# The dt projection with two products per tile, unit 0 taking tiles of h along with it, and three units' weights split ahead of dt's chain

## The chip, the cores and the metric

The kernel runs on one core of one Trainium2 chip. The metric is device time in microseconds (us) for one execution, taken as the median over runs. Engines are named as in the profile: PE (TensorE, matrix products), DVE (VectorE), ACT (ScalarE), POOL (GpSimd) and SP (SyncE, which issues most loads).

## The reference

The program is a trunk of two layers on x of shape 512 tokens by 1024 features, float32. Layer 0 mixes tokens with a Mamba-2 state-space scan, layer 1 with a short gated convolution; each is followed by a gated ConvFFN. Only the start of layer 0 is touched here:

```python
h = rms_norm(x, mix_pre_g[0])
zxbcdt = h @ w_in                       # z | x | B | C | dt (32 heads)
xbc = silu(causal_dwconv(x|B|C, conv_w, conv_b))      # 4 taps
dt = softplus(dt_raw + dt_bias)
a_cs = cumsum(dt * -exp(a_log))         # per head, within chunks
lmat = exp(tril(a_cs_l - a_cs_s))
y = C (B^T x dt)*lmat + C prev * exp(a_cs)            # 8 groups of 4 heads
out = rms_norm((y + x * d) * silu(z)) @ w_out
```

Float32 accuracy is kept by splitting both operands of a large product into a float32r high part and the float32r rest: `three` adds high by high, weight rest by high, and high by h's rest.

## The kernel before

All engines run their own instruction stream, written out by hand; semaphores tie them together, and the order in each stream is the order of the code. Weights are cut into **units** of 128 output columns (or 128 input rows). For each unit SP loads `w_raw` (two buffers), ACT copies it to the high part `w_hi` and DVE subtracts to get the rest `w_lo` (`splits_to(n)` on both engines brings the split up to unit n-1; three slots). PE then runs `unit(u)`: 8 tiles k of h, three products each, into one bank of PSUM, so 24 products of 128x512. SP loads unit u only when `w_lo` of unit u-2 is done.

**The start.** ACT and DVE normalise x (`xn_tok`), PE turns it into feature-major tiles in banks 0 to 5 (`turn_xn`), ACT writes `h_hi` per tile k, DVE `h_lo`. PE then does the dt projection (32 columns of weights, padded with zeros to 128 in `wdt_hi` and `wdt_lo`, three products per tile, bank 7), then unit 0, then unit 1.

**dt's chain.** ACT copies dt's rows out (`dt_row`); `turn_dt` on PE transposes them into token-major form; DVE and ACT compute softplus and a (`dt_u` to `a_tok`, ACT with Abs, Exp and Ln); `turn_acs` on PE multiplies by a triangle to form the cumulative sums; ACT copies them (`acs_row`) and stores them to DRAM; SP loads them back as `acs_b`, the same row on all partitions.

**Group 0.** Units 0 to 5 of a group are B, C, two tiles of x and two tiles of z. For B, C and x, `conv_in` (ACT) copies the bank out and writes the first tap, `conv` (DVE) adds three taps, `conv_out` (ACT) applies Silu. `segments` (DVE) forms the differences of the cumulative sums in `mask`, `exps` (ACT) takes Exp of them, `exps_row` (ACT) Exp of `acs_b` into `e_row`. `mask` times `cbm` on DVE waits for all 7 Exp instructions of the group. PE turns x tiles to token-major form after the Silu of each (L1013), DVE makes `xdt` and `xdd` of them, and PE forms the states from `xdd` (L1020), runs the scan (L1030) and goes on with units 6 and 7. Exp and Silu use different tables of ACT, and the compiler puts an ACT_TABLE_LOAD where the function's table changes.

In unit's argument `behind`, a function is given that PE runs after tile k:

```python
            unit(0, bank[GROUP_BANKS[0]][:], behind={1: turn_dt, 3: turn_pages})
            pe.wait_ge(dt_row_done, 1)
            unit(1, bank[GROUP_BANKS[1]][:], behind={2: turn_acs})
```

Of the kernel before, what the change touches and what calls it, by code (L numbers as in the profile page):

```python
# [5 lines left out]
F32 = mybir.dt.float32  # L6
F32R = mybir.dt.float32r
ALU = mybir.AluOpType
# [7 lines left out]
def build(nc, x, mix_pre_g, mix_post_g, ffn_pre_g, ffn_post_g, ssd_w_in, ssd_conv_w, ssd_conv_b,  # L16
# [129 lines left out]
    SC_BANKS = (2, 3, 4, 5, 6, 7)  # L146
    AHEAD = 3

    acs_dram = nc.dram_tensor("acs_dram", [HEADS, T], F32, kind="Internal").ap()

    ctx = ExitStack()
    with ctx:
        def sb(name, shape, dt=F32, stack=ctx):
            return stack.enter_context(nc.sbuf_tensor(name, shape, dt))
# [28 lines left out]
        with ExitStack() as ssd:  # L183
            acs_b = sb("acs_b", [P, HG, T], stack=ssd)
            mask = sb("mask", [P, HG, T], stack=ssd)
            feat = sb("feat", [P, 4, T], stack=ssd)
            pad = sb("pad", [P, 2, T + P], stack=ssd)
            cbm = sb("cbm", [P, T], stack=ssd)
            b_tok = sb("b_tok", [P, LATER], stack=ssd)
            xdt = sb("xdt", [P, C, HG * HD], stack=ssd)  # L190
            xdd = sb("xdd", [P, C - 1, HG * HD], stack=ssd)
            prev = sb("prev", [P, C - 1, HG * HD], stack=ssd)
            e_row = sb("e_row", [P, XG, LATER], stack=ssd)
            z_act = sb("z_act", [P, XG, T], stack=ssd)
            square, total = sb("square", [P, 2, T], stack=ssd), sb("total", [P, T], stack=ssd)
            few = sb("few", [P, P], stack=ssd)
            decay, c_decay = (few[:, n * HG * C:n * HG * C + HG * (C - 1)].rearrange("p (h c) -> p h c", h=HG) for n in range(2))
            d_col = few[:, 2 * HG * C:2 * HG * C + IT]
            acs_tok, dt_tok = sb("acs_tok", [P, C, HEADS], stack=ssd), sb("dt_tok", [P, C, HEADS], stack=ssd)
            with ExitStack() as late:  # L200
                y_hi, y_lo = sb("y_hi", [P, IT, T], F32R, late), sb("y_lo", [P, IT, T], F32R, late)
            with ExitStack() as start:
                xn_tok = sb("xn_tok", [P, C, D], stack=start)
                pages = sb("pages", [P, 4, P], stack=start)
                wdt_raw = sb("wdt_raw", [P, DT, HEADS], stack=start)
                wdt_hi, wdt_lo = sb("wdt_hi", [P, DT, P], F32R, start), sb("wdt_lo", [P, DT, P], F32R, start)
                dt_row = sb("dt_row", [HEADS, T], stack=start)
                a_log_b, dt_bias_b, d_b = (sb(n, [P, HEADS], stack=start) for n in ("a_log_b", "dt_bias_b", "d_b"))
                sum_sq, r_tok = sb("sum_sq", [P, C], stack=start), sb("r_tok", [P, C], stack=start)
                dt_u, dt_e, a_tok = (sb(n, [P, C * HEADS], stack=start) for n in ("dt_u", "dt_e", "a_tok"))  # L210
                acs_row = sb("acs_row", [HEADS, T], stack=start)

        with ExitStack() as rest:
# [23 lines left out]
            sem(n) for n in ("xn_ready", "xn_turned", "page1_turned", "pages_turned", "par1_done", "par_done"))  # L237
        wdt_cleared, wdt_split, dt_row_mm, dt_row_done = (sem(n) for n in ("wdt_cleared", "wdt_split", "dt_row_mm", "dt_row_done"))
        dt_mm, dt_act, dt_vec, acs_mm, acs_row_done, acs_tok_done, pads_done = (
# [83 lines left out]
        def _(pool):  # L323
# [7 lines left out]
                               pattern=[[1, P]], channel_multiplier=-1).then_inc(consts_done, 1)  # L331
            for part in (wdt_hi, wdt_lo):
                pool.memset(part[:].bitcast(F32)[:, :, HEADS:], 0.0).then_inc(wdt_cleared, 1)
            pool.memset(ones[:], 1.0).then_inc(consts_done, 1)
            pool.memset(total[:], 0.0).then_inc(summed, 1)
            for n in range(IT - 1):
# [5 lines left out]
        def _(act):  # L342
# [22 lines left out]
            act.wait_ge(page1_turned, 1)  # L365
            nc.scalar.copy(par[:, 1, 0:ROWS[1]], bank[6][:, 0:ROWS[1]]).then_inc(par1_done, 1)
            act.wait_ge(par1_done, 1)
            for k in range(DT):
                act.wait_ge(xn_turned, k + 1)
                nc.scalar.activation(h_hi[:, k, :], bank[k % 6][:], ACT.Copy, scale=one(col_gain(MIX_PRE, 0, k))).then_inc(h0_hi_done, 1)  # L370
                if k == 0:
                    act.wait_ge(wdt_landed, 16)
                    act.wait_ge(wdt_cleared, 2)
                    nc.scalar.activation(wdt_hi[:, :, 0:HEADS], wdt_raw[:], ACT.Copy).then_inc(wdt_split, 1)
                if k == 3:
                    splits_to(1)
            splits_to(2)
            act.wait_ge(dt_row_mm, 1)
            nc.scalar.copy(dt_row[:], bank[7][0:HEADS, :]).then_inc(dt_row_done, 1)
            act.wait_ge(pages_turned, 1)  # L380
# [11 lines left out]
            nc.scalar.activation(dt_e[:], dt_e[:], ACT.Ln, bias=1.0).then_inc(dt_act, 1)  # L392
            splits_to(3)
            act.wait_ge(acs_mm, 1)
# [35 lines left out]
            for g in range(GROUPS):  # L430
# [5 lines left out]
                conv_in(g, 2, g * XG)  # L436
                if g == 0:
                    exps(g)
                    exps_row(g)
                conv_in(g, 3, g * XG + 1)  # L440
                conv_out(g, 2)
                act.wait_ge(cb_turned, 2 * g + 2)
                nc.scalar.copy(b_tok[:], bank[3][:, 0:LATER]).then_inc(b_tok_done, 1)
                conv_out(g, 3)
                act.wait_ge(unit_done, GU * g + 5)
                nc.scalar.activation(z_act[:, 0, :], bank[0][:], ACT.Silu).then_inc(evicted, 1)
# [131 lines left out]
        def _(dve):  # L578
# [10 lines left out]
            for c in range(C):  # L589
                dve.wait_ge(r_tok_root, c + 1)  # L590
                nc.vector.reciprocal(r_tok[:, c:c + 1], r_tok[:, c:c + 1]).then_inc(r_tok_done, 1)
                dve.wait_ge(r_tok_done, c + 1)
                nc.vector.tensor_scalar(xn_tok[:, c, :], x_tok[:, c, :], r_tok[:, c:c + 1], None, ALU.mult).then_inc(xn_ready, 1)
            dve.wait_ge(par1_done, 1)
            for k in range(DT):
                dve.wait_ge(h0_hi_done, k + 1)
                nc.vector.scalar_tensor_tensor(out=h_lo[:, k, :], in0=bank[k % 6][:], scalar=one(col_gain(MIX_PRE, 0, k)),
                                               in1=h_hi[:, k, :].bitcast(F32), op0=ALU.mult, op1=ALU.subtract).then_inc(h0_lo_done, 1)
                if k == 0:
                    dve.wait_ge(wdt_split, 1)  # L600
                    nc.vector.tensor_tensor(wdt_lo[:, :, 0:HEADS], wdt_raw[:], wdt_hi[:, :, 0:HEADS].bitcast(F32),
                                            ALU.subtract).then_inc(wdt_split, 1)
                if k == 5:
                    splits_to(1)
            splits_to(2)

# [6 lines left out]
            for h in range(HX):  # L613
# [7 lines left out]
                                           op0=ALU.mult, op1=ALU.mult).then_inc(dt_vec, 1)  # L621
            splits_to(3)
            dve.wait_ge(acs_mm, 2)
# [29 lines left out]
            for g in range(GROUPS):  # L653
                conv(g, 0, CONV_T - 2 * GROUPS + g)
                conv(g, 1, CONV_T - GROUPS + g)
                if not g:
                    segments(g)
                conv(g, 2, g * XG)
                conv(g, 3, g * XG + 1)
# [187 lines left out]
        def _(pe):  # L847
# [94 lines left out]
            for c in range(C):  # L942
# [5 lines left out]
                if c == 1:  # L948
                    pe.wait_ge(page1_landed, 16 * N_PAGE1)
                    nc.tensor.transpose(bank[6][:, 0:ROWS[1]], pages[0:ROWS[1], 1, :], ident[0:ROWS[1], 0:ROWS[1]]).then_inc(page1_turned, 1)  # L950
                if c < C - 2:
                    keep_warm(4, 7)

            pe.wait_ge(wdt_split, 2)
            for k in range(DT):
                pe.wait_ge(h0_lo_done, k + 1)
                last = three(bank[7][:], wdt_hi[:, k, :], wdt_lo[:, k, :], h_hi[:, k, :], h_lo[:, k, :], k == 0, k == DT - 1)
                if k + 6 < DT:
                    for c in range(C):
                        turned = turn_xn(k + 6, c)  # L960
                    turned.then_inc(xn_turned, 1)
            last.then_inc(dt_row_mm, 1)

            def turn_dt():
                pe.wait_ge(dt_row_done, 1)
                for c in range(C):
                    last = nc.tensor.transpose(bank[4][:, c * HEADS:(c + 1) * HEADS], dt_row[:, c * P:(c + 1) * P], ident[0:HEADS, 0:HEADS])
                last.then_inc(dt_mm, 1)
# [14 lines left out]

            pe.wait_ge(par1_done, 1)
            unit(0, bank[GROUP_BANKS[0]][:], behind={1: turn_dt, 3: turn_pages})
            pe.wait_ge(dt_row_done, 1)
            unit(1, bank[GROUP_BANKS[1]][:], behind={2: turn_acs})

            for g in range(GROUPS):
                u = GU * g  # L990
                if g:
                    pe.wait_ge(evicted, GU * g)
                unit(u + 2, bank[GROUP_BANKS[2]][:])
                unit(u + 3, bank[GROUP_BANKS[3]][:])
# [142 lines left out]
```

## Time and profile before

| | |
|---|---|
| median of 3 runs | 1345.62 us (1345.48 to 1346.71) |
| profiled execution | 1345.41 us, of which the span of its core 1343.7 us |
| PE busy | 1332.0 us (99% of the span) |
| DVE busy | 784.3 us (58%) |
| ACT busy | 569.2 us (42%) |
| granted TensorE clock | 1.00 (mean of the core) |

Busy time says how long an engine had an instruction in work, averaged over the whole run. The change touches the first 65 us alone, so the stretches there are to be read one by one.

### The profile page before, as it was taken

Reading aid. Unit: us, or ns where it says so; the run is one execution under the profiler, and the core shown is the slowest. Engines: PE = TensorE matmul, PEld = TensorE weight load, DVE = VectorE, ACT = ScalarE, POOL = GpSimd, SP = SyncE. Lnnn points to the kernel's source line nnn. Section 1 sums busy time; section 2 is a strip of 40 time slices with the busy share of each in tenths; the row PEclk is TensorE's granted clock in tenths of the full one; section 3 lists DMA queues with packets and bytes.
Section 4 is the critical chain, followed back from the end, with each engine's and each line's share of the span. In section 5 each row is a group of like instructions: output and inputs, shape, how many; then the busy total and the mean of one; then the engine's idle time right before and its main releaser. Section 6 shows DMA issues by size and latency. Waiting matters only on the chain.

```text
span 1343.7 us, 15929 instructions
## 1 busy us (share of the span) xinstructions
PE 1332.0 (99%) x6474; PEld 1115.5 (83%) x6474; DVE 784.3 (58%) x1139; ACT 569.2 (42%) x875; POOL 24.8 (2%) x28
## 2 busy tenths in 40 slices
PE   8999999999999999999999999999999999999998
PEld 7888888888888988888888888888898888888886
DVE  4889888888525566656542265445566666654223
ACT  6666655566316434333331173222554433333112
POOL 0000000000000000000000000000000000000000
PEclk9999999999999999999999999999999999999999
DMA  5533233432231233333333313334223333333331
GB/s 151 161 110 92 84 107 110 125 110 90 94 125 54 79 95 109 99 103 96 95 125 112 101 55 94 94 99 128 72 69 106 109 94 96 104 99 126 96 108 63
DMA packets 181773, 135.70 MB, mean 101 GB/s; under 512 B 5645, under 2 KB 169893, under 8 KB 180677
## 3 DMA queue, kind: packets, MB, share of 16 engines
q1 hardware_dynamic: 181653, 134.62, 32.8%
q8 instruction: 51, 0.84, 0.2%
q14 instruction: 21, 0.17, 0.0%
q10 hardware_dynamic: 48, 0.07, 0.0%
HBM read 132.51 MB, written 2.16 MB: 100 GB/s over the span
## 4 chain that ended last, share of the span: by engine, by line
PE 97%; ACT 1%; issue 0%; DVE 0%; DMA 0%; SPq 0%; DVEq 0%; ACTq 0%
PE bank L849 21%; PE bank L851 21%; PE bank L850 21%; PE bank L910 9%; PE bank L911 9%; PE bank L912 9%; PE bank L1030 1%; PE bank L1038 1%; PE bank L1020 1%; PE bank L887 1%; PE bank L1013 1%; PE bank L1002 0%; DMA pages<-in_ssd_norm_w 0%; ACT w_hi L355 0%; ACT h_hi L370 0%
## 5 line engine op out<-in xcount | busy, mean ns | idle before, releaser
L849 PE MATMUL bank<-h_hi,w_hi 128*128 128x512 f32 (+1 forms) x1352 | 513.8, 380 | 0.0
L851 PE MATMUL bank<-h_lo,w_hi 128*128 128x512 f32 (+1 forms) x1352 | 511.1, 378 | 0.0
L850 PE MATMUL bank<-h_hi,w_lo 128*128 128x512 f32 (+1 forms) x1352 | 510.8, 378 | 0.0
L585 DVE TENSOR_TENSOR w_lo<-w_raw,w_hi 128x1024 fp32r<-128x1024 f32 x228 | 286.0, 1257 | 325.8 <-ACT w_hi L355 325.8
L355 ACT ACTIVATE w_hi<-w_raw 128x1024 fp32r<-128x1024 f32 x228 | 238.4, 1053 | 195.3 <-PE bank L912 172.3
L851 PEld LDWEIGHTS bank<-h_lo,w_hi 128*128 128x128 f32 x1352 | 254.2, 188 | 47.4
L850 PEld LDWEIGHTS bank<-h_hi,w_lo 128*128 128x128 f32 x1352 | 254.4, 188 | 46.6
L849 PEld LDWEIGHTS bank<-h_hi,w_hi 128*128 128x128 f32 x1352 | 254.3, 188 | 46.4
L910 PE MATMUL bank<-w_hi,hid_hi 128*128 128x512 f32 x416 | 162.4, 390 | 0.0
L912 PE MATMUL bank<-w_hi,hid_lo 128*128 128x512 f32 x416 | 161.9, 389 | 0.0
L911 PE MATMUL bank<-w_lo,hid_hi 128*128 128x512 f32 x416 | 161.8, 389 | 0.0
L912 PEld LDWEIGHTS bank<-w_hi,hid_lo 128*128 128x128 f32 x416 | 78.1, 188 | 16.3
L910 PEld LDWEIGHTS bank<-w_hi,hid_hi 128*128 128x128 f32 x416 | 78.1, 188 | 16.1
L911 PEld LDWEIGHTS bank<-w_lo,hid_hi 128*128 128x128 f32 x416 | 78.1, 188 | 15.9
L780 DVE SCALAR_TENSOR_TENSOR acc<-cpad,par,acc 128x512 f32<-128x512 f32 x104 | 77.9, 749 | 4.4 <-ACT acc L542 1.8
L645 DVE SCALAR_TENSOR_TENSOR feat<-pad,par,feat 128x512 f32<-128x512 f32 x96 | 71.5, 751 | 13.6 <-ACT feat L407 11.3
L546 ACT ACTIVATE acc<-acc 128x512 f32<-128x512 f32 x44 | 27.9, 634 | 115.8 <-DVE acc L780 115.8
L542 ACT ACTIVATE acc<-cpad,par 128x512 f32<-128x512 f32 x44 | 35.9, 817 | 81.9 <-DVE cpad L793 81.9
L549 ACT ACTIVATE hid_hi<-gated 128x512 fp32r<-128x512 f32 x44 | 27.8, 633 | 81.2 <-DVE gated L802 81.2
L785 DVE TENSOR_TENSOR hid_lo<-gated,hid_hi 128x512 fp32r<-128x512 f32 x52 | 36.0, 693 | 36.4 <-ACT hid_hi L549 30.8
L910 PE MATMUL bank<-w_hi,y_hi 128*128 128x512 f32 x128 | 50.3, 393 | 0.0
L912 PE MATMUL bank<-w_hi,y_lo 128*128 128x512 f32 x128 | 49.9, 390 | 0.0
(146 smaller groups left out, 943.9 us busy)
## 6 DMA issues: line engine op xcount, KB each, us to landing
w_raw<-in_ffn_w_up SPq DMA_DIRECT2D x88, 512.0 KB, 3.7
w_raw<-in_ssd_w_in SPq DMA_DIRECT2D x48, 512.0 KB, 3.9
w_raw<-in_ffn_w_down SPq DMA_DIRECT2D x44, 512.0 KB, 3.5
w_raw<-in_sc_w_in SPq DMA_DIRECT2D x24, 512.0 KB, 3.7
acs_b<-acs_dram SPq DMA_DIRECT2D x8, 1024.0 KB, 6.1
w_raw<-in_ssd_w_out SPq DMA_DIRECT2D x16, 512.0 KB, 3.5
w_raw<-in_sc_w_out SPq DMA_DIRECT2D x8, 512.0 KB, 3.5
x_tok<-in_x SPq DMA_DIRECT2D x4, 512.0 KB, 4.9
```

What stands on the lines that cost most here:

```text
L355: nc.scalar.activation(w_hi[slot(u)][:], w_raw[:, u % 2, :], ACT.Copy).then_inc(w_hi_done, 1)
L542: nc.scalar.activation(acc[:], cpad[:, CW - 1:CW - 1 + T], ACT.Identity, bias=one(col_ffn_b(layer, t)), scale=one(col_ffn_w(layer, CW - 1, ...
L585: nc.vector.tensor_tensor(w_lo[slot(u)][:], w_raw[:, u % 2, :], w_hi[slot(u)][:].bitcast(F32), ALU.subtract).then_inc(w_lo_done, 1)
L645: nc.vector.scalar_tensor_tensor(out=feat[:, f, :], in0=pad[:, f % 2, tap:tap + T], scalar=one(col_ssd_w(tap, page_tile)), in1=feat[:, f, ...
L780: nc.vector.scalar_tensor_tensor(out=acc[:], in0=cpad[:, tap:tap + T], scalar=one(cols(tap)), in1=acc[:], op0=ALU.mult, op1=ALU.add).then_ ...
L785: nc.vector.tensor_tensor(hid_lo[:, t, :], gated[:], hid_hi[:, t, :].bitcast(F32), ALU.subtract).then_inc(hid_lo_done, 1)
L849: nc.tensor.matmul(dst, wh, xh, start=start, stop=False)
L850: nc.tensor.matmul(dst, wl, xh, start=False, stop=False)
L851: return nc.tensor.matmul(dst, wh, xl, start=False, stop=stop)
L910: nc.tensor.matmul(dst[:], in_hi[:, k, toks], hi, start=k == 0, stop=False)
L911: nc.tensor.matmul(dst[:], in_hi[:, k, toks], lo, start=False, stop=False)
L912: last = nc.tensor.matmul(dst[:], in_lo[:, k, toks], hi, start=False, stop=k == b.tiles - 1)
```

## The change

- **dt's product.** High part and rest of dt's weights lie side by side in `wdt` (64 columns, no padding). Per tile PE multiplies `wdt` once with `h_hi` and once with `h_lo`: two products with 64 result rows in place of three with 128. `turn_dt` is now a product of the 64 rows of `dt_row` with `pair`, two identities stacked, made on POOL, which adds the two halves while it transposes.
- **Unit 0 with dt.** PE goes over tiles `at` with dt's two products, and does unit 0's three for tile `at - 2` behind them (`LAG = 2`). The first product of a tile waits for `h_hi` of that tile only. `turn_pages` comes before unit 0's last tile, `turn_dt` behind unit 0, and `turn_acs` moves from the third tile of unit 1 to behind the second tile of unit 2.
- **Splits.** dt's weights are split before h; unit 0's weights behind tile 1 of h on both engines (before: ACT behind tile 3, DVE behind tile 5); units 1 and 2 right behind h. Unit 2's split stood behind dt's Ln and a.
- **Order in group 0.** On DVE the taps of the first x tile come before `segments`. On ACT that tile's Silu comes ahead of the second x tile's `conv_in`, `exps` behind it, and `exps_row` behind the second tile's Silu.
- Four of the warming products (`keep_warm`) at the start are dropped.

```diff
@@ gpsimd
-            for part in (wdt_hi, wdt_lo):
-                pool.memset(part[:].bitcast(F32)[:, :, HEADS:], 0.0).then_inc(wdt_cleared, 1)
             pool.memset(ones[:], 1.0).then_inc(consts_done, 1)
+            pool.wait_ge(consts_done, 5)
+            pool.tensor_tensor(pair[:], ident[:, 0:HEADS], ident[:, HEADS:2 * HEADS], ALU.add).then_inc(pair_done, 1)
@@ scalar
+            act.wait_ge(wdt_landed, 16)
+            nc.scalar.activation(wdt[:, :, 0:HEADS], wdt_raw[:], ACT.Copy).then_inc(wdt_split, 1)
             act.wait_ge(par1_done, 1)
             for k in range(DT):
...
-                if k == 0:
-                    act.wait_ge(wdt_landed, 16)
-                    act.wait_ge(wdt_cleared, 2)
-                    nc.scalar.activation(wdt_hi[:, :, 0:HEADS], wdt_raw[:], ACT.Copy).then_inc(wdt_split, 1)
-                if k == 3:
+                if k == 1:
                     splits_to(1)
-            splits_to(2)
+            splits_to(3)
...
             nc.scalar.activation(dt_e[:], dt_e[:], ACT.Ln, bias=1.0).then_inc(dt_act, 1)
-            splits_to(3)
             act.wait_ge(acs_mm, 1)
...
                 if g == 0:
+                    conv_out(g, 2)
+                conv_in(g, 3, g * XG + 1)
+                if g == 0:
                     exps(g)
-                    exps_row(g)
-                conv_in(g, 3, g * XG + 1)
-                conv_out(g, 2)
+                else:
+                    conv_out(g, 2)
...
                 conv_out(g, 3)
+                if g == 0:
+                    exps_row(g)
@@ vector
-                if k == 5:
+                if k == 1:
                     splits_to(1)
-            splits_to(2)
+            splits_to(3)
...
+                conv(g, 2, g * XG)
                 if not g:
                     segments(g)
-                conv(g, 2, g * XG)
                 conv(g, 3, g * XG + 1)
@@ tensor
-                if c < C - 2:
+                if c == 0:
                     keep_warm(4, 7)
...
-                last = three(bank[7][:], wdt_hi[:, k, :], wdt_lo[:, k, :], h_hi[:, k, :], h_lo[:, k, :], k == 0, k == DT - 1)
...
+            for at in range(DT + LAG):
+                if at < DT:
+                    pe.wait_ge(h0_hi_done, at + 1)
+                    nc.tensor.matmul(bank[7][0:2 * HEADS, :], wdt[:, at, :], h_hi[:, at, :], start=at == 0, stop=False)
+                    pe.wait_ge(h0_lo_done, at + 1)
+                    last = nc.tensor.matmul(bank[7][0:2 * HEADS, :], wdt[:, at, :], h_lo[:, at, :], start=False, stop=at == DT - 1)
...
+                if at >= LAG:
+                    k = at - LAG
...
+                    last = three(bank[GROUP_BANKS[0]][:], hi[:, cols], lo[:, cols], h_hi[:, k, :], h_lo[:, k, :], k == 0, k == DT - 1)
...
+                    if at == DT:
+                        turn_pages()
+            pe.wait_ge(dt_row_done, 1)
+            turn_dt()
+
+            unit(1, bank[GROUP_BANKS[1]][:])
...
-                unit(u + 2, bank[GROUP_BANKS[2]][:])
+                unit(u + 2, bank[GROUP_BANKS[2]][:], behind={1: turn_acs} if g == 0 else {})
```

How it moves instructions is shown at three places. First PE at the start, where dt's products meet the tiles of h. Before, three products per tile, then the transposes of a later tile:

```order
L849 MATMUL bank<-h_hi,wdt_hi 128x512
L850 MATMUL bank<-h_hi,wdt_lo 128x512
L851 MATMUL bank<-h_lo,wdt_hi 128x512
L938 MATMUL bank<-ident,xn_tok 128x128 x4
L849 MATMUL bank<-h_hi,wdt_hi 128x512
```

Now, from tile 1 on to tile 3; `wdt` holds dt's weights, `w_hi` and `w_lo` unit 0's:

```order
L984 MATMUL bank<-h_hi,wdt 64x512
L986 MATMUL bank<-h_lo,wdt 64x512
L939 MATMUL bank<-ident,xn_tok 128x128 x4
L984 MATMUL bank<-h_hi,wdt 64x512
L986 MATMUL bank<-h_lo,wdt 64x512
L850 MATMUL bank<-h_hi,w_hi 128x512
L851 MATMUL bank<-h_hi,w_lo 128x512
L852 MATMUL bank<-h_lo,w_hi 128x512
L984 MATMUL bank<-h_hi,wdt 64x512
L986 MATMUL bank<-h_lo,wdt 64x512
```

Unit 0's products, which came after all of dt's, stand between dt's from the third tile on.

Second ACT in group 0, from the split of a unit's weights behind the first x tile's `conv_in` to the first z tile (L446, now L449). Before:

```order
L417 ACT_TABLE_LOAD
L417 ACTIVATE mask<-mask 128x2048 [waits seg_done]
L418 ACTIVATE few<-few 128x12
L419 ACTIVATE few<-acs_b 128x12
L428 ACTIVATE e_row<-acs_b 64x384 x4
L406 COPY pad<-bank 128x512 [waits conv_step,unit_done]
L407 ACTIVATE feat<-bank,par 128x512
L355 ACTIVATE w_hi<-w_raw 128x1024 [waits unit_done,raw_landed0]
L413 ACT_TABLE_LOAD
L413 ACTIVATE feat<-feat 128x512 [waits conv_step]
L443 COPY b_tok<-bank 128x384 [waits cb_turned]
L413 ACTIVATE feat<-feat 128x512 [waits conv_step]
```

Now, from the Exp of `mask` to the first z tile:

```order
L416 ACT_TABLE_LOAD
L416 ACTIVATE mask<-mask 128x2048 [waits seg_done]
L417 ACTIVATE few<-few 128x12
L418 ACTIVATE few<-acs_b 128x12
L444 COPY b_tok<-bank 128x384 [waits cb_turned]
L412 ACT_TABLE_LOAD
L412 ACTIVATE feat<-feat 128x512 [waits conv_step]
L427 ACT_TABLE_LOAD
L427 ACTIVATE e_row<-acs_b 64x384 x4
L449 ACT_TABLE_LOAD
L449 ACTIVATE z_act<-bank 128x512 [waits unit_done]
```

The Exp of `e_row` stands alone behind the last Silu of x, with a table load before it and one behind it; before, one load served all of the group's Exp instructions.

Third PE around `turn_acs` (L979, now L971: four products into bank 2, and one into bank 3 behind them); `w_hi1` and `w_lo1` are unit 1's weights, `w_hi2` and `w_lo2` unit 2's. Before, within unit 1:

```order
L849 MATMUL bank7<-h_hi,w_hi1 128x512
L850 MATMUL bank7<-h_hi,w_lo1 128x512
L851 MATMUL bank7<-h_lo,w_hi1 128x512
L979 MATMUL bank2<-tri,a_tok 32x128 x4
L982 MATMUL bank3<-a_tok,tri 128x128
L849 MATMUL bank7<-h_hi,w_hi1 128x512
```

Now, from the last tile of unit 1:

```order
L850 MATMUL bank7<-h_hi,w_hi1 128x512
L851 MATMUL bank7<-h_hi,w_lo1 128x512
L852 MATMUL bank7<-h_lo,w_hi1 128x512
L850 MATMUL bank0<-h_hi,w_hi2 128x512
L851 MATMUL bank0<-h_hi,w_lo2 128x512
L852 MATMUL bank0<-h_lo,w_hi2 128x512
L850 MATMUL bank0<-h_hi,w_hi2 128x512
L851 MATMUL bank0<-h_hi,w_lo2 128x512
L852 MATMUL bank0<-h_lo,w_hi2 128x512
L971 MATMUL bank2<-tri,a_tok 32x128 x4
L974 MATMUL bank3<-a_tok,tri 128x128
```

`turn_acs` stood behind three tiles of unit 1; it stands behind all of unit 1 and two tiles of unit 2. On ACT the copy to `acs_row`, which waits for it, still stands ahead of the first `conv_in`.

## Rows read from the trace of the kernel before

**Rows 1.** Stretches: length, each engine's busy us (count), granted clock, DMA share, GB/s

```profile
20.61:26.98 6.37, 6.37 (x32) 5.02 (x31) 0.81 (x5) 3.11 (x9) 0.00 (x0) 1.00 0.50 139
33.99:39.43 5.44, 5.44 (x25) 4.50 (x24) 5.33 (x7) 4.77 (x6) 0.00 (x0) 1.00 0.85 290
63.53:1338.00 1274.47, 1273.60 (x6154) 1067.52 (x6152) 741.75 (x1062) 523.54 (x801) 21.81 (x15) 1.00 0.32 98
```

**Rows 2.** Timeline of ACT and DVE, start: start us, length us, engine, line [idle <-releaser]

```profile
11.59 0.69 ACT L370 ACTIVATE h_hi<-bank,par 128x512 fp32r<-128x512 f32 x1 [1.36 <-PE bank L938]
...
14.19 1.07 ACT L355 ACTIVATE w_hi<-w_raw 128x1024 fp32r<-128x1024 f32 x1
15.14 1.28 ACT L370 ACTIVATE h_hi<-bank,par 128x512 fp32r<-128x512 f32 x2
...
12.38 0.75 DVE L597 SCALAR_TENSOR_TENSOR h_lo<-bank,par,h_hi 128x512 fp32r<-128x512 f32 x1 [1.28 <-ACT h_hi L370]
```

**Rows 3.** Timeline of PE and DVE, dt's chain: turn_dt, a_tok, turn_acs

```profile
22.06 0.43 PE L967 MATMUL bank<-ident,dt_row 32*128 32x32 f32 x4
...
28.89 0.29 DVE L619 SCALAR_TENSOR_TENSOR a_tok<-dt_tok,a_log_b 128x128 f32<-128x128 f32 x1
...
29.24 1.06 PE L979 MATMUL bank<-tri,a_tok 128*32 128x128 f32 x8
```

**Rows 4.** Timeline of ACT in group 0

```profile
30.34 0.58 ACT L395 COPY acs_row<-bank 32x512 f32<-32x512 f32 x1 [0.85 <-PE bank L979]
...
31.41 0.59 ACT L406 COPY pad<-bank 128x512 f32<-128x512 f32 x1 [0.50 <-ACT acs_row L395]
...
32.57 1.06 ACT L355 ACTIVATE w_hi<-w_raw 128x1024 fp32r<-128x1024 f32 x1
...
41.87 1.28 ACT L417 ACT_TABLE_LOAD   x1
43.16 1.92 ACT L417 ACTIVATE mask<-mask 128x2048 f32<-128x2048 f32 x1
...
45.19 2.15 ACT L428 ACTIVATE e_row<-acs_b 64x384 f32<-64x384 f32 x4
...
51.55 0.46 ACT L443 COPY b_tok<-bank 128x384 f32<-128x384 f32 x1
51.91 0.63 ACT L413 ACTIVATE feat<-feat 128x512 f32<-128x512 f32 x1
52.44 0.59 ACT L446 ACTIVATE z_act<-bank 128x512 f32<-128x512 f32 x1
52.92 1.06 ACT L355 ACTIVATE w_hi<-w_raw 128x1024 fp32r<-128x1024 f32 x1
```

**Rows 5.** Timeline of DVE in group 0

```profile
32.80 2.33 DVE L645 SCALAR_TENSOR_TENSOR feat<-pad,par,feat 128x512 f32<-128x512 f32 x3 [1.75 <-ACT feat L407]
35.04 1.22 DVE L585 TENSOR_TENSOR w_lo<-w_raw,w_hi 128x1024 fp32r<-128x1024 f32 x1
36.17 2.32 DVE L645 SCALAR_TENSOR_TENSOR feat<-pad,par,feat 128x512 f32<-128x512 f32 x3
...
39.54 0.17 DVE L631 TENSOR_TENSOR few<-acs_b,acs_tok 128x12 f32<-128x12 f32 x1
39.63 3.22 DVE L636 TENSOR_SCALAR mask<-acs_b,acs_tok 128x128 f32<-128x128 f32 x16
...
52.88 2.29 DVE L666 TENSOR_TENSOR mask<-mask,cbm 128x2048 f32<-128x2048 f32 x1
55.09 1.22 DVE L585 TENSOR_TENSOR w_lo<-w_raw,w_hi 128x1024 fp32r<-128x1024 f32 x1
```

**Rows 6.** Timeline of PE: second x tile turned, states of group 0

```profile
52.59 0.66 PE L1013 MATMUL bank<-ident,feat 128*128 128x128 f32 x4 [0.24 <-ACT feat L413]
...
58.65 1.53 PE L1020 MATMUL bank<-xdd,b_tok 128*128 128x256 f32 x6
```

**Rows 7.** The stretch behind PE's last product, columns as in rows 1

```profile
1338.20:1343.70 5.50, 0.00 (x0) 0.00 (x0) 2.18 (x4) 0.94 (x3) 0.00 (x0) 0.94 0.25 95
```

## What was predicted before the run

> **What bounds the kernel now.** I read the stretches first: from 63.53 us, where unit 6 begins, to 1338 us PE is busy 1273.60 of 1274.47 us [rows 1]. What the change does before 63.53 us is therefore handed on one for one: every later product is in the same order on an engine that has nothing to wait for. Only two questions are left: when PE gets to unit 6, and whether a new wait stands on the way. For these I read the timelines of the three engines. A unit is 24 products in 5.44 us, 0.227 us each [rows 1]. The reader should see in [rows 6] that the second x tile's transposes already wait 0.24 us for ACT's Silu, and in [rows 5, 6] that the states start at 58.65 us, 3.56 us behind the last split before them (55.09 us). So ACT and DVE, though less busy than PE, have almost nothing to spare in group 0; what comes late there, PE waits for.
>
> The sum below follows the changed order from the first tile of h, with durations and gaps between starts from the rows.
>
> **The start, a gain of 1.94 us.** The first h_hi still begins at 11.59 us: it waits for PE's transposes [rows 2], which wait for the same x. ACT has 1.36 us idle before it, and this covers dt's split, moved there. h_hi's follow at 0.59 us (1.28 less 0.69), so the second starts at 12.18 us, and unit 0's w_hi, now behind it, at 12.77 us, done 1.07 us later at 13.84 us. A hand-over from ACT to DVE takes 0.10 us (11.59 + 0.69 to 12.38), from DVE to PE I take 0.05 us. DVE's w_lo starts at 13.94 us and gives way after 1.13 us (35.04 to 36.17 in [rows 5]). The third h_lo is thus done at 13.94 + 1.13 + 0.75 = 15.82 us, and dt's second product of the third tile starts at 15.87 us. From there a tile is five products on PE (1.13 us) against at most 0.75 us on DVE, so PE doesn't wait again. Left are this product, unit 0's 3 of that tile, 5 tiles of 5, and 2 of 3: 35 products, 7.93 us, to 23.80 us. The turns: the stretch of unit 0 is 6.37 us, 0.93 us over its products; 0.43 us of this is `turn_dt` [rows 3], so 0.50 us remains for the pages. `turn_dt` as a true float32 product costs between 0.43 us (its four transposes now) and 1.06 us (the four products of `turn_acs`, eight records); I take the middle, 0.74 us. Unit 1 begins at 25.04 us; it began at 26.98 us, the end of unit 0's stretch.
>
> dt's products: 512 columns stream past 64 weight columns as past 128, so I exclude a gain and take 0.227 us. The nearest row with a narrow weight is L979, with 32 columns: 8 records of 128 columns in 1.06 us, which would be 0.53 us for 512 columns; it is float32 and not float32r, hence no more than a bound. The split of unit 2, taken from the dt chain's end, hides in ACT's and DVE's wait for PE there. The missing warming products and POOL's `pair` cost nothing: PE waits for x at that point.
>
> **The cumulative sums, 2.60 us later.** `turn_acs` doesn't wait for its data: from `turn_dt` to the end of `a_tok` it was 7.12 us (22.06 to 29.18 us [rows 3]), now from 24.30 us, so to 31.42 us at most. But it stands behind unit 1 and two tiles: 25.04 + 5.44 + 1.36 = 31.84 us. `acs_row` came 1.10 us behind its start [rows 3, 4], so at 32.94 us instead of 30.34 us. Queued behind that copy on ACT are all `conv_in`, the splits of units 3 and on, and the Silus. Before, ACT did not wait for unit 0 there but for its own copy [rows 4]; it does so again, 2.60 us later, and unit 0 being done earlier is of no use.
>
> **Unit 3, a wait of 1.7 us.** DVE's first taps, at 32.80 us before, move to 35.40 us; unit 3's w_lo follows 2.24 us later, at 37.64 us, done 38.86 us [rows 5]. PE is through unit 2 at 31.84 + 1.3 (`turn_acs`: 1.06 us [rows 3], and an estimate of 0.24 us, two records more at the same pace, for its second part) + 6 × 0.68 = 37.2 us, and waits until 38.9 us. Unit 3 began at 39.43 us before; the gain has shrunk to 0.52 us.
>
> **The second x tile, a wait of 2.3 us.** On DVE the second taps go from 38.77 us (37.64 + 1.13) to 41.09 us. ACT's Silu of C follows at 41.14 us, the first x tile's `conv_in` 0.53 us later (51.91 to 52.44 [rows 4]) at 41.67 us, and the taps of x 1.39 us after that (31.41 [rows 4] to 32.80 [rows 5]) at 43.06 us, now ahead of `segments`. Then w_lo at 45.30 us, the small difference at 46.43 us, `mask` 46.52 to 49.74 us [rows 5]. `acs_b`, on hand by 39.54 us before [rows 5], comes 2.60 us later and is early. ACT's Exp instructions start at 49.79 us and take 2.03 us without `e_row` (43.16 to 45.19), `b_tok` 0.36 us, the table load for Silu 1.29 us (41.87 to 43.16) [rows 4]: the last Silu starts at 53.47 us, is done at 54.10 us, and the transposes start at 54.15 us instead of 52.59 us [rows 6]. DVE's last taps are done before (about 52 us). PE was ready for them at 52.35 us; with unit 3 0.52 us earlier it is at 51.83 us, and waits 2.3 us. It is now 1.56 us behind.
>
> **The states, a wait of 3.8 us.** Behind that Silu ACT now loads Exp's table (54.00 us), does `e_row` (55.29 us, 2.15 us), loads Silu's table (57.44 us), evicts z (58.73 us) and only then splits unit 7 (0.48 us on, 59.21 us, done 60.27 us) [rows 4]. Before, that split came 1.01 us behind the Silu's start (51.91 to 52.92). The two loads cost 2.58 us, `e_row` 2.15 us, and all of it lies on the path: DVE's product of `mask` waits for `e_row` too (57.5 us, 2.29 us, done before), and w_lo, the x products and `xdd` stand behind. w_lo starts at 60.32 us and the states 3.56 us on, at 63.88 us instead of 58.65 us. PE, done with unit 5 at 54.15 + 0.43 + 5.44 = 60.0 us, waits 3.8 us.
>
> Unit 6 is thus 5.23 us later, and so is the end: all that follows waits for PE, in the old order. 1345.41 us, the profiled execution, becomes 1350.6 us; the median shown is 0.21 us above it: **1350.8 us**. The ledger against before is −1.94 at unit 1, −0.52 at unit 3, +1.56 at the x tile, +5.23 at the states.
>
> **A rule weighed.** ACT's row for a table load ends 1.28 us after its start, and the Exp starts 0.01 us later [rows 4]; I take 1.29 us. The Trainium skill (ScalarE: Activation LUTs, What ACT_TABLE_LOAD costs) adds a drain of 1.38 us to each switch. By it the three switches between the mask's Exp and the z tile would give 4.1 us more, 1354.9 us; the trace disagrees, since no such gap stands around the load.
>
> **The rivals.** (1) *The gain stays*: unit 1 earlier by 1.94 us, a wait of 0.2 us at `turn_acs` gone, nothing new: 1343.5 us. It needs ACT's and DVE's path from `acs_row` to the states shorter by over 7 us than summed; for it speaks only that both engines idle a good share of this stretch, against it that the row at 52.59 us had no slack even before [rows 6]. It decides as soon as PE waits nowhere in group 0. (2) *Less than 0.2% either way*, the hand-overs or the start being better by some 2.6 us than summed. (3) *Narrow products are slow*: 11 of dt's products behind 15.87 us at 0.53 us instead of 0.227 us move everything by 3.3 us, 1354.1 us. (4) *A table switch in this order costs twice its row*: three times 1.29 us, 1354.7 us; no row shows it. (5) *The clock falls in the wait before the states*: the 4.88 us of PE's work up to unit 6 would take up to twice as long, at most 1355.7 us. In the 5.50 us behind PE's last product the mean granted clock is 0.94 [rows 7], that is 1.2 instead of 2.4 GHz for 12% of it, 0.66 us: PE had then done nothing for some 4.8 us, a us more than the wait forecast. The Trainium skill (TensorE: Matmul & The Clock Gate, HAM oscillation) has the clock fall when PE idles between bursts; the trace agrees at its end, and no row shows an idle time as long as this one within the work.
>
> **How the numbers follow.** A run of this kernel can tell a difference of about 0.2%, 2.7 us. The forecast has 0.66: 1349.3 to 1352.3 us, with `turn_dt` at its bounds (0.3 us either way) and some 1.2 us for the hand-overs. Rival 1 has 0.05, rival 2 0.07, rival 3 0.06, rival 4 0.05, rival 5 0.11. The range, 1348.5 to 1354.5 us, leaves out rivals 1 and 2 and the upper part of 4 and 5, less than 0.2 in all. Slower are the forecast and rivals 3 to 5: 0.88; the same 0.07; faster 0.05.
>
> **What would show it.** Right: unit 1 begins near 25.0 us, `acs_row` near 32.9 us, PE waits for w_lo ahead of unit 3, for the Silu of the second x tile and for `xdd`, about 1.7, 2.3 and 3.8 us, and unit 6 begins near 68.8 us at clock 1.00. Wrong: products of dt more than 0.3 us apart, an `acs_row` before 31 us, or a wait before the states under 1 us.

## The result, and the profile after

The changed kernel takes 1353.03 us (median of 6 runs, 1352.67 to 1353.82) against 1345.70 us for the kernel before (6 runs taken beside it): 7.3 us more, ratio 1.0055, 95% interval of the ratio 1.0044 to 1.0065. The forecast was 1350.8 us, in a range from 1348.5 to 1354.5 us. The profiled execution took 1353.68 us, 8.27 us more than the one before the change.

What PE waits for, as the view of its waits lists it for the changed kernel (engine, line, what was waited for: us in total, times, longest us):

```profile
PE bank L1040 <- DVE xdd L678: 3.9, 1, 3.9
PE bank L1033 <- ACT feat L412: 2.3, 1, 2.3
...
PE bank L850 <- DVE w_lo L588: 1.5, 1, 1.5
PE bank L951 <- DMA pages<-in_ssd_norm_w: 1.1, 1, 1.1
```

The three waits that were forecast are there: for the states' input (3.8 us forecast), for the second x tile's Silu (2.3 us) and for unit 3's rest (1.7 us). The fourth stands before h, and comes from loads that landed late in this execution.

Where they stand in time, in PE's timeline of the changed kernel (start us, length us, engine, line):

```profile
17.71 0.39 PE L984 MATMUL bank<-h_hi,wdt 128*64 128x512 f32 x1
17.94 0.39 PE L986 MATMUL bank<-h_lo,wdt 128*64 128x512 f32 x1
18.17 0.40 PE L850 MATMUL bank<-h_hi,w_hi 128*128 128x512 f32 x1
...
25.25 1.07 PE L958 MATMUL bank<-pair,dt_row 64*128 64x32 f32 x8
26.25 0.50 PE L850 MATMUL bank<-h_hi,w_hi 128*128 128x512 f32 x1
...
33.28 1.06 PE L971 MATMUL bank<-tri,a_tok 128*32 128x128 f32 x8
...
40.35 0.50 PE L850 MATMUL bank<-h_hi,w_hi 128*128 128x512 f32 x1 [1.47 <-DVE w_lo L588]
...
55.59 0.66 PE L1033 MATMUL bank<-ident,feat 128*128 128x128 f32 x4 [2.32 <-ACT feat L412]
...
65.61 2.90 PE L1040 MATMUL bank<-xdd,b_tok 128*128 128x256 f32 x6 [3.90 <-DVE xdd L678]
...
71.82 0.48 PE L850 MATMUL bank<-h_hi,w_hi 128*128 128x512 f32 x1
```

Unit 1 begins at 26.25 us, 0.73 us earlier than before; unit 3 at 40.35 us, 0.92 us later; the second x tile is 3.00 us behind [rows 6], the states 6.96 us [rows 6], unit 6, at 71.82 us, 8.29 us. After that nothing is added.

The way to the states on ACT and DVE in the changed kernel, to be laid beside [rows 4, 5]:

```profile
12.53 1.27 ACT L374 ACTIVATE h_hi<-bank,par 128x512 fp32r<-128x512 f32 x2 [1.04 <-PE bank L939]
...
34.38 0.58 ACT L394 COPY acs_row<-bank 32x512 f32<-32x512 f32 x1 [3.95 <-PE bank L971]
...
53.61 1.28 ACT L412 ACT_TABLE_LOAD   x1
54.91 0.63 ACT L412 ACTIVATE feat<-feat 128x512 f32<-128x512 f32 x1
55.55 1.28 ACT L427 ACT_TABLE_LOAD   x1
56.85 2.17 ACT L427 ACTIVATE e_row<-acs_b 64x384 f32<-64x384 f32 x4
59.04 1.28 ACT L449 ACT_TABLE_LOAD   x1
60.33 0.60 ACT L449 ACTIVATE z_act<-bank 128x512 f32<-128x512 f32 x1
60.96 1.06 ACT L357 ACTIVATE w_hi<-w_raw 128x1024 fp32r<-128x1024 f32 x1
...
62.05 1.23 DVE L588 TENSOR_TENSOR w_lo<-w_raw,w_hi 128x1024 fp32r<-128x1024 f32 x1 [0.64 <-ACT w_hi L357]
```

ACT waits 3.95 us for `turn_acs`, with unit 0's result long in its bank. Behind the last Silu (54.91 us) the split of unit 7 takes 6.05 us to begin, against 1.01 us before [rows 4].

One thing is new. The stretches of the changed kernel with unit 1, and from the states to unit 6 (columns as in rows 1; the granted clock is the third number from the end):

```profile
26.25:31.70 5.45, 5.45 (x25) 4.52 (x25) 1.14 (x6) 3.62 (x6) 0.00 (x0) 1.00 0.01 4
65.61:71.82 6.21, 6.12 (x50) 4.91 (x51) 3.17 (x8) 2.61 (x3) 0.00 (x0) 0.77 0.16 48
```

From the states to unit 6 the mean clock is 0.77, and the stretch is 6.21 us long instead of 4.88 us (58.65 to 63.53 us before).

### The profile page after: what moved, and what is told of

Read it like the earlier page. It is cut to its first block, busy times and chain, and to the rows that moved or that the text cites. A ratio compares the mean times of both kernels' runs of the same rounds, so it can differ in the third digit from the quotient of the medians.

```text
span 1352.0 us, 15905 instructions
## 1 busy us (share of the span) xinstructions
PE 1332.5 (99%) x6462; PEld 1114.7 (82%) x6462; DVE 784.2 (58%) x1139; ACT 571.7 (42%) x877; POOL 23.7 (2%) x27
## 4 chain that ended last, share of the span: by engine, by line
PE 96%; DVE 1%; ACT 1%; DMA 0%; issue 0%; SPq 0%; DVEq 0%; ACTq 0%
PE bank L852 21%; PE bank L850 21%; PE bank L851 21%; PE bank L911 9%; PE bank L912 9%; PE bank L913 9%; PE bank L1050 1%; PE bank L1058 1%; PE bank L1040 1%; PE bank L888 1%; DVE feat L646 0%; DMA x_tok<-in_x 0%; PE bank L1022 0%; PE bank L1033 0%; DVE w_lo L588 0%
```

## The experiments

The first four ask where the loss comes from. Theory: three waits in group 0, made by the late `turn_acs` and by the order of group 0. Rival: the start (narrow products, `turn_dt` as a true product, x later). Differences from the changed kernel compare runs that were not taken side by side: the kernel before took 1345.70 us beside it, and 1345.48 and 1345.44 us beside the experiments.

**The old order of group 0 in the changed kernel.**

```diff
 # ACT, g == 0
-  conv_out(2); conv_in(3); exps; b_tok; conv_out(3); exps_row
+  exps; exps_row; conv_in(3); conv_out(2); b_tok; conv_out(3)
 # DVE, g == 0
-  conv(2); segments; conv(3)
+  segments; conv(2); conv(3)
```

> The changed kernel, with the order of group 0 on ACT and DVE as before the change; start, turn_acs and splits stay as changed. My theory (the waits of group 0 make the loss): the wait before the states, 3.9 us in the changed kernel, goes to under 0.5 us and the clock stays at 1.00 there (another 1.3 us), while the waits for unit 3's w_lo and for the x tiles stay or grow to some 3.3 us together at the x tiles, because e_row again stands ahead of the Silus: 3.0 to 4.3 us below the changed kernel, 1348.7 to 1350.0 us. Rival (the start makes the loss: narrow products, float32 turn_dt, x later): no change, 1353 us.

Measured: 1349.49 us (9 runs, ratio to before 1.0028, interval 1.0018 to 1.0038), 3.5 us below the changed kernel. PE's waits, and the two stretches around the wait for the first x tile:

```profile
PE bank L1029 <- ACT feat L412: 2.9, 2, 2.7
...
PE bank L846 <- DVE w_lo L584: 1.5, 1, 1.5
```

```profile
51.50:54.30 2.80, 0.12 (x2) 0.01 (x1) 2.73 (x4) 2.77 (x4) 0.00 (x0) 1.00 0.31 93
54.30:58.53 4.23, 3.99 (x14) 3.23 (x15) 4.20 (x4) 2.27 (x4) 0.00 (x0) 0.60 0.57 170
```

The wait for `xdd` has left the list, that for unit 3 stayed at 1.5 us, as the theory has it. With the wait gone the clock is 1.00 from the states to unit 6, as expected, but the fall moved instead of going away: the clock is 0.60 behind the wait of 2.7 us for the x tile, which the theory did not have.

**The new order alone, in the kernel before.** The reverse of the edit above.

> The kernel before with the changed order of group 0 on ACT and DVE alone. My theory: the two more table loads and e_row stand between the last Silu and unit 7's split, so PE waits about 3.8 us for xdd before the states and about 1 us at the second x tile: 4.2 us above the kernel before, and up to 1.3 us more if the clock falls in that wait, 1349.9 to 1351.2 us. Rival (the start makes the loss): 1345.7 us.

Measured: 1351.77 us (4 runs, ratio 1.0046, interval 1.0031 to 1.0061), 6.3 us above the kernel before, 0.6 us over the upper end of what was expected. Waits of PE and the stretch from the states to unit 6:

```profile
PE bank L1024 <- DVE xdd L681: 3.9, 1, 3.9
...
PE bank L1017 <- ACT feat L413: 0.9, 1, 0.9
```

```profile
62.99:69.34 6.35, 6.35 (x51) 5.36 (x51) 4.00 (x12) 2.61 (x3) 0.00 (x0) 0.73 0.17 48
```

With the old start the same wait of 3.9 us appears, and the same fall of the clock, worth 1.47 us (6.35 less 4.88). The rival expected no change.

**`turn_acs` in unit 1.**

```diff
-            unit(1, bank[GROUP_BANKS[1]][:])
+            unit(1, bank[GROUP_BANKS[1]][:], behind={6: turn_acs})
-                unit(u + 2, bank[GROUP_BANKS[2]][:], behind={1: turn_acs} if g == 0 else {})
+                unit(u + 2, bank[GROUP_BANKS[2]][:])
```

> The changed kernel with turn_acs behind the seventh tile of unit 1 instead of the second tile of unit 2. My theory: acs_row and all behind it on ACT come 2.0 us earlier (three tiles of 0.68 us), the wait ahead of unit 3 is gone, the one before the states stays at some 3.8 us: 2.0 us below the changed kernel, 1351.0 us. Rival (the start makes the loss, or the order of group 0 alone): 1353 us.

Measured: 1351.33 us (4 runs from 1350.66 to 1352.83, ratio 1.0043, interval 1.0028 to 1.0058), 1.7 us below the changed kernel. In its timeline `acs_row` comes 2.17 us earlier (0.12 us of it because h began earlier, at 12.41 us), and PE no longer waits ahead of unit 3; the wait for `xdd` is unchanged:

```profile
32.21 0.58 ACT L394 COPY acs_row<-bank 32x512 f32<-32x512 f32 x1 [1.91 <-PE bank L971]
```

```profile
PE bank L1040 <- DVE xdd L678: 3.9, 1, 3.9
PE bank L1033 <- ACT feat L412: 2.1, 1, 2.1
```

The profiled execution is the slowest of the four: its stretch from the states to unit 6 is 7.49 us long, against 6.21 us in the changed kernel's profile (the row is in the last section). So the 1.7 us, the difference of two medians, holds an unknown share of the clock.

**Warming products in the wait before the states.** The products' results are not used.

```diff
                 unit(u + 5, bank[GROUP_BANKS[5]][:])
+                if g == 0:
+                    keep_warm(13, 7)
```

> The changed kernel with 13 products of float32, 128x128, into a free bank behind unit 5 of group 0, some 3 us of work in the wait of 3.9 us before the states; their results are not used. If the clock's fall in that wait costs PE's work from the states to unit 6 its 1.3 us: granted clock 1.00 in that stretch, 4.9 us long instead of 6.2 us, 1.3 us below the changed kernel, 1351.7 us. If the stretch is long for another reason (the data of the states, the evictions): 6.2 us again and 1353 us.

Measured: 1351.71 us (4 runs, ratio 1.0044, interval 1.0027 to 1.0060), 1.3 us below the changed kernel. The stretches from the states to unit 6, and behind the wait for the second x tile:

```profile
65.03:69.84 4.81, 4.69 (x52) 4.04 (x51) 3.17 (x8) 2.61 (x3) 0.00 (x0) 1.00 0.13 36
54.70:58.50 3.80, 3.80 (x13) 3.18 (x14) 0.28 (x1) 3.69 (x6) 0.00 (x0) 0.59 0.49 135
```

With PE at work in the wait the clock is 1.00 and the stretch 4.81 us long: the 1.4 us were the clock's. In this execution it fell in the x tile's wait instead (2.34 us), where it had held in the changed kernel's (2.32 us). That delays unit 5 alone, and PE had the wait for `xdd` before it anyway.

**Both put back**: the first and the third edit together.

> The changed kernel with both put back: the order of group 0 on ACT and DVE as before the change, and turn_acs behind the seventh tile of unit 1. What stays is the start (narrow products, unit 0 along with dt, earlier splits) and turn_dt behind unit 0. My theory: the old order gave 1349.5 us; turn_acs three tiles earlier takes 2.0 us more off, and the clock's fall (some 1.3 us in that run) may go with the wait of 2.7 us that it followed: 1346.2 to 1347.5 us, so still not below the kernel before, since turn_dt stands 3.2 us later than there. Rival (one of the two alone carries the loss, the other adds nothing): 1349 us or more.

Measured: 1346.95 us (10 runs, ratio 1.0010, interval 1.0001 to 1.0019), within the expected 1346.2 to 1347.5 us and 1.5 us above the kernel before. The two edits take off 6.1 us together, 3.5 and 1.7 us singly, so neither carries the loss alone. PE waits 2.4 us at the x tiles here, and the clock falls there as well, so the fall that might have gone with that wait stayed:

```profile
52.25:55.90 3.65, 3.65 (x13) 3.11 (x14) 3.62 (x4) 2.28 (x4) 0.00 (x0) 0.53 0.49 126
```

**e_row directly behind the mask's Exp.**

```diff
                 if g == 0:
                     exps(g)
+                    exps_row(g)
...
                 conv_out(g, 3)
-                if g == 0:
-                    exps_row(g)
```

> The changed kernel with e_row directly behind the mask's Exp, so that one table load serves both and none stands between the last Silu and the z tile. My theory: the two loads (2.6 us) leave the way to the states, and e_row's 2.15 us move ahead of the last Silu: the wait for xdd is gone, the wait at the second x tile goes from 2.3 to some 4.5 us, 1.7 us below the changed kernel, 1351.3 us with the clock falling in that wait as it did before the states. If table loads cost nothing there: 1353 us.

Measured: 1351.08 us (4 runs, ratio 1.0044, interval 1.0030 to 1.0058), 1.95 us below the changed kernel. The wait for `xdd` is gone and the x tile's is 4.6 us, as summed; the clock fell again:

```profile
PE bank L1032 <- ACT feat L412: 4.6, 1, 4.6
```

```profile
56.74:60.06 3.32, 3.32 (x10) 2.80 (x11) 1.91 (x3) 1.37 (x2) 0.00 (x0) 0.53 0.67 276
```

**The start kept, the way of the sums cleared.** What differs from the changed kernel:

```diff
 # PE
-            turn_dt behind unit 0
+            turn_dt behind turn_pages, ahead of unit 0's last tile
-                unit(u + 2, ..., behind={1: turn_acs} if g == 0 else {})
+            unit(1, bank[GROUP_BANKS[1]][:], behind={5: turn_acs})
 # ACT
-  acs_row; store; conv_in(0); conv_in(1)
+  conv_in(0); acs_row; store; conv_in(1)
-  conv_out(2); conv_in(3); exps; b_tok; conv_out(3); exps_row
+  exps; conv_in(3); exps_row; conv_out(2); conv_out(3); b_tok
 # DVE
-  acs_tok; conv(0); conv(1); conv(2); segments; conv(3)
+  conv(0); acs_tok; conv(1); segments; conv(2); conv(3)
```

> The changed kernel's start, and the way of the cumulative sums cleared: turn_dt behind tile 6 of unit 0, turn_acs behind the sixth tile of unit 1, the first conv_in (ACT) and its taps (DVE) ahead of acs_row and acs_tok, the old order of group 0 but with the second x tile's conv_in between the mask's Exp and e_row, and its Silu ahead of b_tok. By the rows' sum PE waits some 0.8 us at the x tiles and nowhere before the states: 1.9 us below the kernel before, 1343.8 us, clock 1.00 up to the end. If the start's gain can't be had at all: 1345.5 us.

Measured: 1343.35 us (11 runs from 1343.01 to 1344.31, ratio 0.9984, interval 0.9975 to 0.9993): 2.1 us below the kernel before and 9.7 us below the changed one. PE's wait at the x tiles, and the stretches before and behind it up to unit 6:

```profile
PE bank L1036 <- ACT feat L414: 0.4, 1, 0.4
```

```profile
11.80:50.64 38.84, 37.11 (x181) 29.10 (x178) 28.44 (x53) 31.44 (x48) 0.00 (x0) 1.00 0.44 124
50.64:61.95 11.31, 11.19 (x82) 9.46 (x83) 7.97 (x13) 5.49 (x8) 0.00 (x0) 1.00 0.54 181
```

Unit 6 begins at 61.95 us instead of 63.53 us, and the clock is 1.00 in both stretches. The new start is worth having once ACT and DVE deliver in time. From the first `h_hi` to unit 6 the recast kernel takes 50.15 us, the kernel before 51.94 us (11.59 to 63.53 us); PE is busy 48.30 and 49.73 us of it by the profiles, so 1.4 us of the 1.8 us gained is work that PE no longer has, and 0.4 us is waiting.

## Why the prediction was right, and where it was short

The direction, the three waits and their causes came out as forecast; the end did not come 5.2 us later but 7.3 us. By its steps:

- **The start, −1.94 us forecast, −0.73 us in the profile.** Two terms differ. h began at 12.53 us, not 11.59 us, since the third quarter of x and the first parameter page landed late in this execution: 0.94 us. That need not come from the change: in the changed start's other profiles h begins at 11.38 to 11.80 us in five and at 12.41 us in one. It may be why the profiled execution is 0.65 us above its median; no other execution of this kernel has a profile. And `turn_dt` took 1.00 us (25.25 to 26.25), near the upper bound of 1.06 us, not the 0.74 us taken: 0.26 us. dt's products follow at 0.23 us (17.71, 17.94, 18.17), so rival 3, slow narrow products, is out.
- **The cumulative sums, +2.60 us forecast, +4.04 us.** 1.20 us of the difference is the start's; the rest is `turn_acs` beginning at 33.28 us, 0.23 us behind 26.25 + 5.44 + 1.36. The mechanism, a copy queued ahead of all `conv_in`, was shown by moving `turn_acs` alone (`acs_row` 2.17 us earlier and 1.7 us less time, for three tiles of 0.68 us) and by the recast version, where the first `conv_in` is ahead of that copy.
- **The waits, 1.7, 2.3 and 3.8 us forecast: 1.47, 2.32 and 3.90 us.** From the last Silu to unit 7's split 5.74 us were summed and 6.05 us came: the load began 0.64 us behind the Silu's start, when the Silu (0.63 us) was done, instead of 0.53 us behind it, and the split 0.63 us behind the z tile's start instead of 0.48 us [rows 4]. Why the split came later, no run shows.
- **A load is 1.28 us.** From the load's start to the next function's it is 1.29 to 1.30 us at all three places, so rival 4, and the drain that the Trainium skill adds (ScalarE: Activation LUTs, What ACT_TABLE_LOAD costs), are out here too; the order with two loads fewer gained 1.95 us, with `e_row` and the clock in it.
- **The clock, left out of the sum, 1.33 us.** This is the largest term that was missing: the sum put it at nothing. Rival 5 had it at a chance of 0.11 and came beside the forecast, not in its place: 6.21 us instead of 4.88 us from the states to unit 6. I had taken from [rows 7] that some 4.8 us without work leave the clock up; that row is one case and gives no limit.

Together: 5.23 + 0.26 + 0.23 + 0.29 (6.05 less 5.74, and rounding) + 1.33 = 7.34 us, and 0.94 us more in the profiled execution. That this meets the 7.33 us between the medians so closely is luck: of the clock's part the five runs without a profile show only the mean of the whole run (0.996 to 0.998, where 0.001 stands for 2.7 us at the lower level), and the profiles of other kernels have it from 1.33 to 2.6 us for the same wait of 3.9 us. Rival 1, the gain stays, was out by 9.5 us for the order as written; the recast version shows its condition, that PE hardly waits in group 0.

Open is what part of the start's gain belongs to the narrow products and what to the earlier splits: they were not tried apart. The count points to the products: dt has 16 instead of 24, which at 0.227 us is 1.82 us less, and `turn_dt` takes 0.57 us more (1.00 against 0.43 us). Open too is what the order on ACT and the order on DVE in group 0 each cost: of these only `e_row` on ACT was moved by itself.

## What to carry to other kernels

An engine that is busy all the time sets the end only while the others hand over in time: a step that saves it 2 us is worth nothing if the copy that everything else queues behind moves back by more (here by 3.1 us: 4.04 us less the 0.94 us by which h was late). When a step is moved, look at what stands behind its consumer in that engine's queue, and at which function table is loaded there: two table changes with 2.2 us of work between them, between a release and the next, made the wait of 3.9 us, with the old start as with the new, and the order that holds them cost the kernel before 6.3 us by itself. A new wait on TensorE has a second price, its clock behind it; work that would be late anyway can hide that price, as unit 5 did with the warming products.

## What was not expected of the hardware

The clock fell to its lower level (0.50, 1.2 GHz) after shorter waits than the 3.8 us I had thought safe, and not always. Of PE's waits in these profiles, those of 2.1 and 2.3 us were followed by a clock of 1.00 in two kernels, and those of 2.3, 2.4 and 2.7 us by 0.59, 0.53 and 0.60 over the next 3.7 to 4.2 us in three others; each of 3.9 us and more without work in it was followed by a fall. The same wait, 3.9 us before the states, cost 1.33 us in one kernel (the changed one), 1.47 us in a second (the new order alone), and in the third (`turn_acs` in unit 1) 2.6 us (stretch of 7.49 us at a mean of 0.62):

```profile
63.45:70.94 7.49, 7.49 (x50) 6.31 (x51) 4.00 (x12) 2.61 (x3) 0.00 (x0) 0.62 0.18 49
```

Single microseconds of three of these cases: the changed kernel behind its wait of 2.3 us (1.00), `turn_acs` in unit 1 behind its wait of 2.1 us (1.00), and the changed kernel behind its wait of 3.9 us (0.50):

```profile
56.00:57.00 1.00, 1.00 (x7) 0.84 (x6) 0.00 (x0) 0.99 (x2) 0.00 (x0) 1.00 0.95 271
54.00:55.00 1.00, 1.00 (x6) 0.82 (x6) 0.00 (x0) 0.99 (x2) 0.00 (x0) 1.00 1.02 305
66.00:67.00 1.00, 1.00 (x3) 0.76 (x3) 0.00 (x0) 0.00 (x0) 0.00 (x0) 0.50 0.55 163
```
